# Two gated linear attentions in one fused block: inner loops moved from two engines to VectorE, and chunk states from 32-row TensorE tiles

## The reference, cut to what matters

```python
LA_BLOCK = 16

def gla_chunked(q, k, v, log_a, scale):
    b, h, s, dk = q.shape
    dv = v.shape[-1]
    c = LA_BLOCK
    n = s // c
    ...
    G = jnp.cumsum(log_a.reshape(b, h, n, c, dk), axis=3)
    rel = jnp.where(causal[:, :, None], G[:, :, :, :, None, :] - G[:, :, :, None, :, :], -jnp.inf)
    a_intra = jnp.einsum('bhnrd,bhnsd,bhnrsd->bhnrs', q, k, jnp.exp(rel))
    o_intra = jnp.einsum('bhnrs,bhnse->bhnre', a_intra, v)
    g_last = G[:, :, :, -1]
    q_in = q * jnp.exp(G)
    k_out = k * jnp.exp(g_last[:, :, :, None, :] - G)
    a_chunk = jnp.exp(g_last)

    def step(state, inp):
        qi, ki, vi, ai = inp
        o = jnp.einsum('bhcd,bhde->bhce', qi, state)
        state = state * ai[..., None] + jnp.einsum('bhcd,bhce->bhde', ki, vi)
        return state, o
    ...
    return (o_intra + jnp.moveaxis(o_inter, 0, 2)).reshape(b, h, s, dv)
```

## Time and profile before

| | us |
|---|---|
| median of 3 runs | 2032.79 |
| lowest and highest | 2029.93, 2032.88 |
| span of the profiled execution | 2027.6 |
| its PE busy | 1944.1 (96%) |
| its DVE busy | 1011.3 (50%) |
| its ACT busy | 763.5 (38%) |
| its POOL busy | 327.8 (16%) |

### The profile page before, as it was taken

One profiled execution on the slowest core, in us unless ns is written; L12 is line 12 of the kernel. 1 busy time (PEld: TensorE's weight loads), 2 busy tenths in 40 slices (PEclk: granted clock), 3 DMA queues, 4 the chain that ended last, 5 costly groups with the idle time before them and its releaser, 6 DMA issues.

```text
span 2027.6 us, 25343 instructions
## 1 busy us (share of the span) xinstructions
PE 1944.1 (96%) x8769; PEld 1555.9 (77%) x8769; DVE 1011.3 (50%) x1417; ACT 763.5 (38%) x1095; POOL 327.8 (16%) x278
## 2 busy tenths in 40 slices
PE   7989987779999999999999999999999999999998
PEld 6779855556788888888878888888776678888887
DVE  5463478765576774334544443433466544434322
ACT  5532554335444443232234322322455443233222
POOL 0051056540211111100011111101000021111100
PEclk9999999889999999999999999999999999999999
DMA  6310110011233333333333333333322023333332
GB/s 184 84 32 2 52 32 12 20 58 34 87 98 98 93 96 93 95 91 104 93 91 96 94 93 102 92 94 93 91 72 59 21 87 100 93 95 100 88 93 70
DMA packets 309219, 161.23 MB, mean 80 GB/s; under 512 B 12688, under 2 KB 306832, under 8 KB 309024
## 3 DMA queue, kind: packets, MB, share of 16 engines
q1 hardware_dynamic: 308080, 157.64, 26.8%
q0 software_dynamic: 640, 2.17, 0.3%
q10 hardware_dynamic: 432, 0.52, 0.1%
HBM read 158.21 MB, written 2.10 MB: 79 GB/s over the span
## 4 chain that ended last, share of the span: by engine, by line
PE 89%; DVE 4%; ACT 3%; issue 3%; SPq 0%; POOL 0%; DMA 0%; DVEq 0%; ACTq 0%; POOLq 0%
PE ps L365 25%; PE ps L367 25%; PE ps L366 25%; PE ps L1031 2%; PE ps L1431 1%; PE ps L1019 1%; PE ps L1627 1%; PE ps L1452 1%; PE ps L1439 1%; PE ps L1913 1%; PE ps L1914 1%; DVE mx L1488 1%; PE ps L1618 1%; DVE mx L1343 0%; PE ps L876 0%
## 5 line engine op out<-in xcount | busy, mean ns | idle before, releaser
L365 PE MATMUL ps<-xhi,whi 128*128 128x512 f32 x1656 | 664.0, 401 | 10.1 <-DVE xlo L437 6.7
L367 PE MATMUL ps<-xhi,wlo 128*128 128x512 f32 x1656 | 646.4, 390 | 0.0
L366 PE MATMUL ps<-xlo,whi 128*128 128x512 f32 x1656 | 645.9, 390 | 0.0
L352 ACT ACTIVATE whi<-raw 128x1024 fp32r<-128x1024 f32 (+2 forms) x297 | 308.9, 1040 | 728.5 <-PE ps L367 725.8
L360 DVE TENSOR_TENSOR wlo<-raw,whi 128x1024 fp32r<-128x1024 f32 (+2 forms) x293 | 361.7, 1235 | 287.7 <-ACT whi L352 287.6
L365 PEld LDWEIGHTS ps<-xhi,whi 128*128 128x128 f32 x1656 | 312.0, 188 | 81.7 <-issue 4.5
L366 PEld LDWEIGHTS ps<-xlo,whi 128*128 128x128 f32 x1656 | 312.1, 188 | 67.6 <-issue 5.6
L367 PEld LDWEIGHTS ps<-xhi,wlo 128*128 128x128 f32 x1656 | 311.7, 188 | 65.8
L594 DVE TENSOR_TENSOR zS<-ps,rs 128x512 f32<-128x512 f32 x132 | 91.3, 692 | 293.5 <-PE ps L367 284.4
L365 PE MATMUL ps<-h_hi,whi 128*128 128x512 f32 x528 | 209.3, 396 | 0.0
L366 PE MATMUL ps<-h_lo,whi 128*128 128x512 f32 x528 | 209.3, 396 | 0.0
(11 more groups left out here) (323 smaller groups left out, 1953.0 us busy)
## 6 DMA issues: line engine op xcount, KB each, us to landing
raw<-in_conv_ffn_w SPq DMA_DIRECT2D x52, 512.0 KB, 3.7
raw<-in_mla_ffn_w SPq DMA_DIRECT2D x52, 512.0 KB, 3.7
raw<-in_w_up SPq DMA_DIRECT2D x44, 512.0 KB, 3.7
raw<-in_w_in SPq DMA_DIRECT2D x28, 512.0 KB, 3.6
raw<-in_conv_w_in SPq DMA_DIRECT2D x24, 512.0 KB, 3.7
raw<-in_w_down SPq DMA_DIRECT2D x16, 448.0 KB, 3.5
raw<-in_conv_ffn_w SPq DMA_DIRECT2D x16, 448.0 KB, 3.6
raw<-in_mla_ffn_w SPq DMA_DIRECT2D x16, 448.0 KB, 3.5
```

What stands on the lines that cost most here:

```text
L352: a.activation(whi[:, u % PARTS, 0:n], raw[:, u % RAW, 0:n], ACT.Copy).then_inc(hi_split, 1)
L365: t_.matmul(out, wh, xh, start=first, stop=False)
L366: t_.matmul(out, wh, xl, start=False, stop=False)
L367: return t_.matmul(out, wl, xh, start=False, stop=last)
```

## The change

1. POOL does nothing in the three passes but `pool_la_setup`, now called for all three ahead. `t{j}`, both value tiles' adds, four `split_lo` (units 26 to 29) and two gates (`mix6`, `mix7`) are now DVE's.
2. `la_spread` is gone, and with it the constant `cmask`. Instead ACT writes the transposed values twice (`act_chunk_parity`): once with the tokens of even chunks, once with those of odd chunks (constant `pmask`), zeros elsewhere.
3. The chunk states come from `chunk_states(r)`, r = 0 to 3, called in rounds 1 to 4 of the inner loop. For token tile t and each head one matmul takes only the 32 token rows 32r to 32r+31 (two chunks), the head's 32 or 64 key columns as weights, and 128 moving columns (64 values of even, 64 of odd chunks). gla has 16 such matmuls in a round, hg 8. ACT copies each r's bank in one instruction, 4 in a pass where there were 16 or 8.
4. The states' scan moves from round 3 to round 8 of DVE's loop, the products have three buffers (`PROD`) instead of two, a result is taken two rounds after its product instead of one, and the hung-in work moves to later rounds.

```diff
-        def la_spread(eng, e, nm, n, engine):
...
-        def pool_la(pool, nm, before, also):
...
+        def act_chunk_parity(act, nm, vi, x):
+
+            for odd in range(2):
+                name = "paired" if nm == "gla" else "taken"
+                a.activation(mx[:, VP + 2 * vi + odd, :], x, ACT.Copy, scale=C("pmask")[:, odd:odd + 1]).then_inc(
+                    *step("act", f"{nm} v{vi} {name}" if odd else f"{nm} v{vi} even"))
...
+            def chunk_states(r):
+                out = pe_ring(pe, f"{nm} kv{r}")
+                toks = slice(32 * r, 32 * r + 32)
...
                 for t in range(TT):
-                    out = pe_ring(pe, f"{nm} kv{n}")
-                    pe.wait_ge(*after(f"{nm} spread{n}"))
-                    pe.wait_ge(*after(f"{nm} ko taken"))
-                    t_.matmul(out, mx[:, KOT, t * P:(t + 1) * P], mx[:, VX[n % 4], :], start=True,
-                              stop=True).then_inc(*step("pe", f"{nm} kv{n} full"))
-                    n += 1
+                    for row, vi, r0 in L["heads"]:
+                        at = t * P + row
+                        pairs = mx[toks, VP + 2 * vi:VP + 2 * vi + 2, t * P + r0:t * P + r0 + DH]
+                        last = t_.matmul(out[row:row + L["dk"], t * P:(t + 1) * P].rearrange("p (two d) -> p two d", two=2),
+                                         mx[toks, KOT, at:at + L["dk"]], pairs, start=True, stop=True)
+                last.then_inc(*step("pe", f"{nm} kv{r} full"))
...
+            for j in range(LC + 3):
+                if j == 8:
                     dve.wait_ge(*after(f"{nm} chunk decays"))
-                    dve.wait_ge(*after(f"{nm} kv{4 * n_heads - 1} taken"))
+                    dve.wait_ge(*after(f"{nm} kv3 taken"))
                     v.tensor_tensor_scan(KVw, AXw, KVw, 0.0, ALU.mult, ALU.add).then_inc(*step("dve", f"{nm} states"))
                 if j < LC:
...
+                    if j >= 3:
+                        dve.wait_ge(*after(f"{nm} intra{j - 3} {nv - 1} full"))
+                    v.tensor_tensor(narrow(PROD[j % 3], LC - j), decayed(j)[:, :, j:LC], k[:, :, 0:LC - j],
+                                    ALU.mult).then_inc(*step("dve", f"{nm} prod{j}"))
+                if j + 1 < LC:
+                    if j:
+                        dve.wait_ge(*after(f"{nm} prod{j - 1}"))
+                    v.tensor_tensor(chunks(mx[:, TJ[(j + 1) % 2], :])[:, :, j + 1:LC], decayed(j)[:, :, j + 1:LC],
+                                    ax[:, :, 1:LC - j], ALU.mult).then_inc(*step("dve", f"{nm} t{j + 1}"))
+                if nv == 1 and 4 <= j:
+                    add(j - 3)
+                if 2 <= j < LC + 2:
+                    weigh(j - 2)
+                    if nv == 2 and j >= 3:
+                        add(j - 2)
                 also(j)
...
-            pool_la_setup(pool, "gla")
-            pool.wait_ge(*after("gdn o7 full"))
...
+            for nm in LA:
+                pool_la_setup(pool, nm)
```

More of the change, by code:

```diff
@@ L1402, in act_la @@
             L = LA[nm]
-            n = 0
-            for h, (row, vi, r0) in enumerate(L["heads"]):
-                rows = slice(row, row + L["dk"])
-                dst = KVw.rearrange("p (d c) -> p c d", c=NL)
-                for t in range(TT):
-                    bank = full(act, f"{nm} kv{n}").rearrange("p (c d) -> p c d", d=DH)
-                    a.activation(dst[rows, 8 * t:8 * t + 8, :], bank[rows, :, :], ACT.Copy).then_inc(
-                        *step("act", f"{nm} kv{n} taken"))
-                    n += 1
+            dst = KVw.rearrange("p (d t r two) -> p r t two d", t=TT, r=4, two=2)
+            for r in range(4):
+                bank = full(act, f"{nm} kv{r}").rearrange("p (t two d) -> p t two d", t=TT, two=2)
+                a.activation(dst[:, r], bank, ACT.Copy).then_inc(*step("act", f"{nm} kv{r} taken"))
             act.wait_ge(*after(f"{nm} q_in"))
@@ L1468, in dve_la_setup, with dve_la, narrow, decayed @@
             v.tensor_tensor(mx[:, QI, :], L["q"], mx[:, PP, :], ALU.mult).then_inc(*step("dve", f"{nm} q_in"))
[L1470 removed]
+        def dve_la(dve, nm, also):
             L = LA[nm]
             n_heads, nv = len(L["heads"]), len(L["v"])
[L1474 to L1477 removed]
+            ax, k = chunks(L["a"]), chunks(L["k"])
+            def narrow(x, n):
+                return x[:, 0:NL * n].rearrange("p (n c) -> p n c", c=n)
+            def decayed(j):
+                return chunks(L["q"] if j == 0 else mx[:, TJ[j % 2], :])
+            def partial(j, vi):
+                return narrow(mx[:, TMP + (vi if nv == 2 else j % 2), :], LC - j)
+            def weigh(j):
+                for vi in range(nv):
+                    if nv == 2 and j == 1:
+                        dve.wait_ge(*after(f"{nm} v{vi} paired"))
+                    if j >= 4 - nv:
+                        dve.wait_ge(*after(f"{nm} o{j - 3 + nv} {vi}"))
+                    dst = chunks(L["o"][vi]) if j == 0 else partial(j, vi)
+                    v.tensor_tensor(dst, narrow(full(dve, f"{nm} intra{j} {vi}"), LC - j),
+                                    chunks(L["v"][vi])[:, :, 0:LC - j],
+                                    ALU.mult).then_inc(*step("dve", f"{nm} intra{j} {vi} taken"))
+            def add(j):
+                for vi in range(nv):
+                    dve.wait_ge(*after(f"{nm} intra{j} {vi} taken"))
+                    o3 = chunks(L["o"][vi])[:, :, j:LC]
+                    v.tensor_tensor(o3, o3, partial(j, vi), ALU.add).then_inc(*step("dve", f"{nm} o{j} {vi}"))
+            for j in range(LC + 3):
+                if j == 8:
@@ L2313, in _ @@
             act_gdn_oT(act)
+            for vi in range(2):
+                act.wait_ge(*after(f"gla v{vi} taken"))
+                act_chunk_parity(act, "gla", vi, mx[:, TMP + vi, :])
             act_la(act, "gla")
@@ L2408, in _ @@
             dve_gdn_chunks(dve, 15, in_chunks)
-            for n in (0, 2):
-                la_spread(dve, v, "gla", n, "dve")
             split_lo(dve, 24)
             dve_hg_silu(dve, 7)
-            dve_la(dve, "gla", in_gla, "hg0")
-            dve_la(dve, "hg0", in_hg0, "hg1")
+            dve.wait_ge(*after("gdn kv7 taken"))
+            dve_la(dve, "gla", in_gla)
+            dve_la(dve, "hg0", in_hg0)
             dve_la(dve, "hg1", in_hg1)
```

145 lines of the change are left out of this document (37 added, 108 removed).

## The result

The changed kernel takes 2003.57 us (median of 4 runs, 2001.58 to 2004.5); the kernel before, beside it on the same chip, 2031.36 (2025.62 to 2032.88). The ratio is 0.9867, 95% interval 0.985 to 0.9884: 27.8 us or 1.3% faster. The profiled spans are 2001.7 and 2027.6 us.

What follows compares the result with a forecast made beforehand. DVE was taken to bound the loops, PE the stretches between. Gains of 23.5 us less 4.5 for clock net 19: span 2027.6 to 2008.6, plus 5.2 gives 2014. Own range 2008 to 2022; 8 in 10, 2000 to 2034.

Steps and rivals of the forecast that it cites:

- the first rival: Chunk-state tiles run at once in the array, so they almost vanish from PE: 2002 us, chance 0.2.
- Entry: Start of gla: no spread stands before its first product, which starts at 269.2 instead of 279.58; gain 10.4 us.
- Gla's loop: Gla's rounds: DVE has 43.7 us of work and idles 8 waiting for PE; 51.7 us, a loss of 2.1.
- the tile's price: PE time of a small chunk-state matmul in gla: at most 0.113 us a record, less if four run at once; middle taken.
- Gla to hg0: Stretch between these loops: 8.2 us instead of 11.0, from PE's 62 state records and the last four adds; gain 2.8.
- hg0 to hg1: Stretch between these loops, 13.3 us before: 7.0 for PE and 0.9 for the adds; gain 5.4 us.
- Hg0's loop: Hg0's rounds: 34 us of DVE work plus 3 of PE delay by chunk states, 37 against 40.1; gain 3.1.
- Hg1: Hg1's loop and end: DVE work 30.5, waits in fox's norms 6, states 7.6, taken as 44.5 us; gain 3.9.
- The clock: Allowance over the passes: 4.5 us taken off the gains for a low granted clock.
- The second: Rival: PE falls to half clock on the small tiles; 2039 us, up to 25 more if both hg loops follow; chance 0.11.
- The third: Rival: DVE becomes the chain, 217 loop instructions pay 0.1 us more each; no change, 2032 to 2035; chance 0.09.
- the price list: DVE instruction costs, start to start: 0.06 us plus 0.034 for each 32 columns, with side work priced separately.

Runs made afterwards that it cites:

- experiment 5: Changed kernel with GpSimd again making the decayed queries and adding gla's second value tile, small tiles kept: 2008.95 us.
- experiment 7: Changed kernel with matmuls between states and decayed queries run two groups at a time, alternating between two column tiles: 1993.99 us.
- experiment 4: Changed kernel with chunk-state matmuls taking all 128 key columns as weights and all 128 token rows: 2017.9 us.
- experiment 2: Changed kernel with each chunk-state matmul contracting over all 128 token rows instead of 32, the head's own columns kept: 2002.8 us.
- experiment 8: Changed kernel with the gated norm of the delta rule's output taken in gla's round 8 instead of 7: 2002.07 us.
- experiment 11: Changed kernel with filler sums keeping TensorE busy in its waits in gla, hg0 and hg1: 1998.54 us.
- experiment 1: Changed kernel with each chunk-state matmul taking all 128 key columns as weights instead of its head's 32 or 64, still 32 rows: 2032.0 us.
- experiment 3: Changed kernel with every round of chunk states computed twice in a row into the same bank: 2019.95 us, ten runs in two groups.

## Why the prediction was right, and where its steps were off

The direction was right and the time, 2003.6, lies in the range for 8 in 10, 2000 to 2034. It is 10.4 us below the forecast of 2014, outside the forecast's own 2008 to 2022, and beside the 2002 of the first rival. So the wide range was right, and the middle of it was not. Step by step:

- **Entry, 10.4 forecast, 10.4 measured** (15.96 to 5.55). It is the spreads' time: experiment 5 kept it with GpSimd at work again.
- **Gla's loop, -2.1 forecast, -0.4 measured.** VectorE's work was 45.0 us (43.7 forecast), its idle time 5.0 and not 8. The step that failed is the tile's price: I took the middle between 0.113 us and a quarter. It is the quarter in gla, the half in hg. The reason I gave for the middle, that the 0.113 of narrow records might be set by loading weights, does not hold: in experiment 7 records with the same 64 columns of weights go from 0.113 to 0.06 us only because neighbours use different columns of the array, and with all 128 (experiment 4) a record takes 0.12, hardly more than with 64. Of the idle time 3.7 us are the wait for gdn's norm, as forecast. The Trainium skill, TensorEngine Tiling (Array Packing), Key Properties, says that different tiles work in parallel: in these traces this holds between column tiles, and experiment 2 shows that row tiles add nothing when the instructions of one row group come in a run. Of the drain at a change of mode, which the same section states, the rows show none: sums, small tiles and the unit's products follow each other without a gap, as far as modelled ends can tell.
- **Gla to hg0, 2.8 forecast, 2.5 measured; hg0 to hg1, 5.4 and 5.5.** TensorE's 62 records of 0.113 set both, as said.
- **Hg0's loop, 3.1 forecast, 1.2 measured.** VectorE worked 34.9 of 38.9 us, near the 34. The rest are waits for TensorE's sums: 1.5 us in rounds 3 and 4, at full clock and behind the chunk states (the line at 345.01), and 2.3 behind round 13, at the lower clock (366.84). The chunk states, for which I had put 3 us of delay, take 1.09 each round; the waits at the end stood in no term.
- **Hg1, 3.9 forecast, 6.8 measured.** I kept 6 us of waits in fox's norms. They are gone (398.64). A likely reason, argued and not tested by itself, is the order: TensorE's sums of squares were one round ahead of VectorE's norm (4 and 5, 6 and 7) and now are two (6 and 8, 8 and 10), and ahead of the first norm the states' scan, 4.4 us, lies in between as well. In gla the edit went the other way, from two rounds to one, and there a wait of 3.7 us is found; moving the norm behind the scan took it away (experiment 8). The sum of this term was also off: 30.5, 6 and 7.6 are 44.1, not 44.5.
- **The clock, 4.5 forecast, about nothing measured.** The mean clock of the six stretches before was 0.69 to 1.00 and now is 0.82 to 1.00; from 265 to 425 us 0.90 became 0.89. The stages' measured gains hold what the clock cost in them and add up to the whole difference, so no separate loss is left. The low clock is not free: the fillers of experiment 11 won some 4 to 5 us on this kernel. But it was there before as well, and its share did not grow, which the allowance took for granted. Nor was the reading behind it right: the stretch at 0.74 that it names as one with little work had TensorE busy for 13.30 of 13.30 us.
- **Sum.** 26.0 us in the passes against 23.5, and no 4.5 off: these two are the 7 us by which 19 was too little. The rest of the 10.4 is what lies around the span: 1.9 us now, where I had 5.2. That 5.2 set the span of the one profiled execution against the median of three; beside the experiments each run of the kernel before took 2.1 to 2.2 us more than its own span.

The rivals: the first came true, for its mechanism and within 1.6 us of its time; a chance of 0.2 was low for the only reading with a reason in the code, that heads write different partitions. The second, half clock on the small tiles, does not happen at 1.08 us a round. Something like it is real: experiment 1 and half of the runs of 3 fell into it, and 4 against 1 shows that 32 rows are part of the cause there. That the overlap saved this change, because it makes the stretches short, is my reading; gla in experiment 3 had stretches twice as long and kept its clock. The third is refuted, VectorE's narrow instructions follow each other by 0.13 us as before. Of the signs, GpSimd's busy time fell by 98 us (85 forecast), and gla's first product came at 271.21, not 269.2, with the stages ahead 2.0 us later. Rounds 0 to 4 lasted 17.6 us (271.95 to 289.57), below the 20 to 25 of the forecast and not under the 15 of the rival, since 1.8 of them are the first sums at half clock.

That VectorE could take over GpSimd's work was right: its busy time in the loops came out at 45.0, 34.9 and 31.8 us, each about 1 us above the price list, and was 44.1, 34.3 and 30.3 before. Giving the work back costs 5.4 us. Of the 28 us, some 5 are this half of the change by that one experiment. The rest is the chunk states', with their spreads (18.4 at the entry and between the passes), and the places that steps have in the rounds.

## What to carry to other kernels

Where many small matmuls write different columns of the array, issue them in turn over the column groups and read the price off the trace: two groups halved it (0.113 to 0.055 us), four quartered it (0.026). Moving work to the engine that ends last can win when the helper shares its memory, but count the waits for the helper apart from the instructions drawn out. And before a saved wait is booked, look at the clock in what follows TensorE's idle stretch: a later norm won 3.4 us in gla and 2.5 of them were lost in hg0, where the clock was lower in that execution, and useless sums in the waits won 8 us.

## What the runs showed of the hardware that was not expected

- Float32 records of 128 moving columns: 0.113 to 0.12 us alone, about half of that with two column tiles and a quarter with four, whether they use 32 or 128 rows. Records of 64 columns of weights and 64 moving columns: 62 in 7.11 us one behind the other, 3.80 when neighbours use different column tiles.
- Records with 32 rows and 128 columns, without overlap, brought a mean granted clock of 0.76 over 18 us although TensorE had no gap; with 128 rows it was 1.00. Records of 32 rows and 64 columns, sent twice, ran at half clock for 33 us in one profile.
- Idle time did it too: after 3.9 us of waiting the next sums ran at half clock, and with 2.7 us of fillers in that wait they did not.
- Beside each of four GpSimd splits one VectorE product ended just after the split, even when it needs 0.28 us alone; two other instructions beside the same split kept their time (0.41 and 0.38 us).
